# Expert weights in transfers of two chunks instead of one, into the same ring of six slots

## The reference

```python
g, idx = lax.top_k(jnp.swapaxes(aff, 1, 2), cap)
xs = jax.vmap(lambda hb, ib: hb[ib])(h, idx)
a = jnp.einsum("becd,edf->becf", xs, w_gate)
u = jnp.einsum("becd,edf->becf", xs, w_up)
y = jnp.einsum("becf,efd->becd", jax.nn.silu(a) * u, w_down) * g[..., None]
```

## Time and profile before

| | us |
|---|---|
| median of 3 runs | 2307.16 (2306.68 to 2309.15) |
| the profiled execution | 2308.26 |
| its span, first to last instruction | 2306.4 |
| expert stage, first copy to last | about 764 to 2260 |
| TensorE busy | 2116.9 (92%) |
| VectorE busy | 1661.5 (72%) |
| ScalarE busy | 1267.0 (55%) |
| GpSimd busy | 249.9 (11%) |

### The profile page before, as it was taken

How to read it: one execution, slowest core, us unless ns; L and a number is a source line. 1 busy time by engine, 2 the same in 40 slices (tenths; PEclk the granted TensorE clock), 3 DMA queues, 4 the chain that set the end, 5 groups by cost and what they waited for, 6 DMA issues and landing times.

```text
span 2306.4 us, 26811 instructions
## 1 busy us (share of the span) xinstructions
PE 2116.9 (92%) x10228; PEld 1456.2 (63%) x10228; DVE 1661.5 (72%) x1617; ACT 1267.0 (55%) x1271; POOL 249.9 (11%) x100
## 2 busy tenths in 40 slices
PE   7989999897873799999999999999999999999992
PEld 7956576665663466666666666666666666666661
DVE  5013251516333789899899998998989989999885
ACT  0012231404003677777777777777777777777771
POOL 0000000000000202202112021120220211202100
PEclk9989999999885899999999999999999999999996
DMA  6851010101121699999999999999999999999992
GB/s 245 327 191 60 23 59 25 75 9 62 56 97 67 256 384 377 363 398 365 382 387 364 393 371 368 401 362 390 378 365 395 366 378 395 363 390 373 373 353 97
DMA packets 95273, 638.97 MB, mean 277 GB/s; under 512 B 11169, under 2 KB 14400, under 8 KB 21184
## 3 DMA queue, kind: packets, MB, share of 16 engines
q1 hardware_dynamic: 90048, 617.55, 69.0%
q0 software_dynamic: 5120, 19.98, 2.9%
HBM read 619.08 MB, written 18.40 MB: 276 GB/s over the span
## 4 chain that ended last, share of the span: by engine, by line
issue 46%; POOL 9%; DMA 7%; PE 4%; DVE 1%; ACT 0%; POOLq 0%; DVEq 0%; ACTq 0%
DMA place<-x_rows,place 6%; POOL place L889 3%; POOL place L897 2%; POOL acc_rows L901 2%; POOL place L887 2%; PE ps L948 1%; PE ps L943 1%; PE ps L944 1%; PE ps L960 0%; PE ps L965 0%; PE ps L961 0%; DVE place L1034 0%; DVE place L175 0%; DVE place L1059 0%; DVE place L1060 0%
## 5 line engine op out<-in xcount | busy, mean ns | idle before, releaser
L1034 DVE TENSOR_TENSOR place<-ring,place 128x2048 fp32r<-128x2048 f32 x528 | 1283.3, 2436 | 110.2 <-ACT place L995 102.3
L995 ACT ACTIVATE place<-ring 128x2048 fp32r<-128x2048 f32 x528 | 1012.4, 1918 | 373.4 <-PE ps L948 232.8
L943 PE MATMUL ps<-place 128*80 128x512 f32 x1408 | 560.4, 398 | 2.4 <-ACT place L995 2.4
L944 PE MATMUL ps<-place 128*80 128x512 f32 x1408 | 552.8, 393 | 0.0
L948 PE MATMUL ps<-place 128*80 128x512 f32 x1408 | 380.6, 392 | 0.9 <-DVE place L1034 0.9
L948 PEld LDWEIGHTS ps<-place 128*80 128x80 f32 x1408 | 208.2, 148 | 117.0 <-DVE place L1034 2.1
L960 PE MATMUL ps<-place 128*80 128x512 f32 x704 | 280.0, 398 | 0.0
L961 PE MATMUL ps<-place 128*80 128x512 f32 x704 | 276.3, 392 | 0.0
L943 PEld LDWEIGHTS ps<-place 128*80 128x80 f32 x1408 | 208.4, 148 | 107.2 <-issue 3.2
L944 PEld LDWEIGHTS ps<-place 128*80 128x80 f32 x1408 | 209.1, 149 | 104.1 <-issue 0.5
L965 PE MATMUL ps<-place 128*80 128x512 f32 x704 | 191.1, 393 | 0.0
(11 more groups left out here) (138 smaller groups left out, 1702.3 us busy)
## 6 DMA issues: line engine op xcount, KB each, us to landing
ring<-in_w_exp SPq DMA_DIRECT2D x528, 1024.0 KB, 6.9
ring<-in_w_ada SPq DMA_DIRECT2D x24, 1024.0 KB, 6.2
place<-in_w_in SPq DMA_DIRECT2D x12, 1024.0 KB, 6.8
bias_scratch<-place POOLq DMA_DIRECT2D x4, 1024.0 KB, 7.5
ring<-in_w_out SPq DMA_DIRECT2D x4, 1024.0 KB, 4.8
place<-bias_scratch SPq DMA_DIRECT2D x4, 1024.0 KB, 4.8
place<-in_xT SPq DMA_DIRECT2D x1, 2560.0 KB, 22.5
place<-in_x SPq DMA_DIRECT2D x1, 2560.0 KB, 9.4
```

Of the source, the lines that this page charges most:

```text
L943: eng.matmul(out, xH[:, e % 2, kk, :], w, start=(kk == 0), stop=False)
L944: eng.matmul(out, xL[:, e % 2, kk, :], w, start=False, stop=False)
L995: eng.activation(wH[:, n % SPLITS, :], ring[:, (FIRST_EXPERT_CHUNK + n) % RING, :], ACT.Copy).then_inc(wh_done, 1)
L1034: eng.tensor_tensor(wL[:, n % SPLITS, :], ring[:, (FIRST_EXPERT_CHUNK + n) % RING, :], wH[:, n % SPLITS, :].bitcast(F32), ALU.subtract).th ...
```

## The change

Expert chunks are issued in pairs: one DMA of 2 MB fills slots s and s+1, 16 KB in each partition. Since 28 is even and the ring has six slots, a pair's slots are always 4 and 5, 0 and 1, or 2 and 3. The pair waits until both slots are free, that is until chunk n+1-6 has been used, and its landing is told by one semaphore, that of the first slot; whoever waits for either chunk waits for it. Everything else about ring, slots and users stays. The host lays a pair's chunks side by side for each partition. Block 1 now issues the first pair (28, 29), block 3 two pairs, block 4 the rest. As an expert has 33 chunks, pairs begin at even p in even experts and at odd p in odd ones, and piece 32 of an even expert is paired with piece 0 of the next.

```diff
-            src = chunk_source(n) if n < FIRST_EXPERT_CHUNK else a["w_exp"][n - FIRST_EXPERT_CHUNK]
-            eng.dma_start(ring[:, n % RING, :], src).then_inc(landed[n % RING], 16)
+            eng.dma_start(ring[:, n % RING, :], chunk_source(n)).then_inc(landed[n % RING], 16)
+
+        def issue_pair(eng, n):
+
+            eng.wait_ge(chunk_used, n + 1 - RING + 1)
+            s = n % RING
+            eng.dma_start(ring[:, s:s + 2, :].rearrange("p s n -> p (s n)"), a["w_exp"][(n - FIRST_EXPERT_CHUNK) // 2]
+                          ).then_inc(landed[s], 16)
 
         def arrived(eng, n):
+            if n >= FIRST_EXPERT_CHUNK:
+                n -= n % 2
             eng.wait_ge(landed[n % RING], 16 * (n // RING + 1))
...
-                for n in range(RING, ADA_CHUNKS + RING):
+                for n in range(RING, FIRST_EXPERT_CHUNK):
                     issue(eng, n)
+                issue_pair(eng, FIRST_EXPERT_CHUNK)
...
-                for n in range(ADA_CHUNKS + RING, ADA_CHUNKS + RING + OUT_CHUNKS):
-                    issue(eng, n)
+                for n in range(FIRST_EXPERT_CHUNK + 2, FIRST_EXPERT_CHUNK + RING, 2):
+                    issue_pair(eng, n)
...
-                for n in range(ADA_CHUNKS + RING + OUT_CHUNKS, FIRST_EXPERT_CHUNK + EXPERT_CHUNKS):
-                    issue(eng, n)
+                for n in range(FIRST_EXPERT_CHUNK + RING, FIRST_EXPERT_CHUNK + EXPERT_CHUNKS, 2):
+                    issue_pair(eng, n)
...
-    w_exp = np.concatenate([gate_up, down], axis=1).reshape(EXPERT_CHUNKS, P, CW)
+    w_exp = np.concatenate([gate_up, down], axis=1).reshape(EXPERT_CHUNKS // 2, 2, P, CW)
+    w_exp = w_exp.transpose(0, 2, 1, 3).reshape(EXPERT_CHUNKS // 2, P, 2 * CW)
```

## The result

The changed kernel takes 2350.4 us (median of 4 runs, 2345.3 to 2358.1) against 2307.3 before: ratio 1.0188, 95% interval 1.0159 to 1.0217. It is 43 us slower, where I had forecast 7 and a range up to 2334. The profiled execution is the longest of the four, 2358.05 with a span of 2356.2, 49.8 over that of before.

What follows compares the result with a forecast made beforehand. TensorE was taken to bound the expert stage, with no steady-state gain; thin-place stalls summed to 4 to 12 us, taken as +7: 2308.3 + 7 = 2315 profiled, median 2314, range 2304 to 2334.

Steps and rivals of the forecast that it cites:

- What bounds the kernel: Expert stage: TensorE busy all 93.3 us of an expert period, never waiting for weights, so the steady-state gain is nothing.
- Against 5.9 us in the quiet part that is just covered: worth 0 there.: Outside the thin place: some 5 us of lost earliness for a pair's first chunk costs 0, split buffers absorbing 2 us.
- the fourth rival: "The DMA queues become the bound": expert-stage queue holes cost 45 us, 2352; chance 0.08; sign: copies wait in all thirds.
- The thin place: A third into each expert, after scatter and gather, at the hidden product's turn: stalls 0.5 to 1.1 us even, 0 to 0.6 odd.
- The rate of 0.53: In the thin place: VectorE's subtraction runs at 2.28/4.27 = 0.53 of its speed while GpSimd's L889 runs.
- the third rival: "Nothing is given back": GpSimd starts after the stalled subtraction, so thin-place lateness counts in full, 23 us, 2330; chance 0.13.
- The gather: GpSimd's fetch of 80 rows per expert: 16 KB ring rows delay it 0 to 1.5 us, bounds 0 and 5.6.
- the other bound for a pair alone: Landing of a 2 MB pair on a quiet queue: 7.2 us taken, 8.4 with the other bound on the rate.
- The ends that held: Expert 0, the w_in load and the last expert, which has no gather: cost 0; for expert 0 at most 1 us.
- Half as many issues: Sync queue: 528 issues of 0.33 us become 264, worth 0 because that queue waits 1308.4 us anyway.

Runs made afterwards that it cites:

- without arithmetic: Changed kernel with GpSimd's three products and sums cut to 16 of 1024 columns, not computing the reference's values: 2307.3 us, ratio 0.9999.
- its control: Kernel before with GpSimd's three products and sums cut to 16 of 1024 columns, not computing the reference's values: 2300.3 us, ratio 0.9968.
- late issue: Kernel before, single 1 MB transfers, but both of a pair issued only when both slots are free: 2309.8 us, ratio 1.0011.
- late arrival: Kernel before, single 1 MB transfers issued as slots free, but the copy of a pair's first chunk waits for the second's landing: 2309.8 us, ratio 1.0008.
- both late: Kernel before, single 1 MB transfers, issued when both slots are free and first chunk copied only when both have landed: 2344.1 us, ratio 1.0168.
- product first: Hidden product put ahead of VectorE's subtraction, silu ahead of ScalarE's copy: in the changed kernel 2347.7 us (1.0172), in the kernel before with four slots 2395.7 (1.0371).
- without rows: Changed kernel with GpSimd's scatters, and gathers from the third on, replaced by DMAs of 64 bytes a row, not computing the reference's values: 2315.4 us, 1.0037.

## Why the prediction was wrong

*What bounds the kernel* was right: nothing to gain in the steady state, and so was the place in the changed kernel. In the profiled run 26.4 of the 30.3 us of stalls, and all six stretches of half clock, lie directly behind piece 10, at the turn named in the earlier trace rows. With runs of 8 KB, where the gather lands earlier, six of nine stalls lie behind piece 8 instead.

*The step that failed* is "Against 5.9 us in the quiet part that is just covered: worth 0 there." It set a loss of 5.3 us of earliness against a cover that was itself computed with the median landing, left 0.6, and called this enough. It should have asked whether the loop with both effects in it still turns faster than TensorE. My own numbers had it: a pair's landing is the old 6.9 with another 2.5 for its second megabyte, 9.4, and not the 7.2 of a pair alone on the queue; measured 9.7 (and 7.4 at least). With 6.6 to 7 us from the landing to the second subtraction's end that is 16.0 to 16.7 of 17.0. The pair thus came late before the disturbance began: the copies waited in 47 of the 48 thirds of an expert, which I had put down as the sign of the fourth rival.

*The thin place* was priced at 0 to 1.1 us, measured up to 3.6 at one wait. I let GpSimd's slowing of VectorE give most of the lateness back, since a late subtraction would fall behind it. Some came back: the 528 subtractions take 1258.7 us and not 1283.3, 24.6 less, some 1.7 us for each of experts 1 to 14. But in each of these one subtraction was still slowed by 1.5 to 2.0 us, where before two were (1.7 and 2.0), and in expert 5 both were. The rate of 0.53 that I used does not fit the rows, which show the engines taking turns by whole operations. The gather came later too, after 13.3 us in the median instead of 9.6, 3.7 later where I took 0 to 1.5 and allowed 5.6. In expert 5 that is the third rival's mechanism, "nothing is given back"; the loss does not need it, as the next paragraph shows.

*The gather* shows one more term. It lands after 12.8 to 13.9 us in three kernels with runs of 16 KB (changed, eight slots, without arithmetic) and after 9.3 to 10.5 in the eight with 8 KB and the old order of products (before and its control, the 2 MB transfer in two runs, late issue, late arrival, both late, five slots, four slots). With the product first it is 15.6 (16 KB) and 12.1 (8 KB, four slots). The plainest pair is the changed kernel with 13.3 and the same with runs of 8 KB with 10.3: the length of the runs holds the gather back. The queue that carries the weights moves its bytes in 52032 packets in the first and 85824 in the second. That fits the Trainium skill, "DMA: Bandwidth & Descriptors", section "Queues, rings and completion order", by which a DMA engine changes between queues only after a whole packet. But it decided nothing: with 8 KB runs the loss was the same, and with eight slots and a gather nearly as late (12.8) there was none.

*The clock* was not in the sum: some 15 of the 49.8 us of the profiled run are TensorE at half clock behind its stalls.

*A slip in the sum,* without effect: the other bound for a pair alone is 4.7 + 3.1 = 7.8 us and not 8.4, which took the fixed part of one bound and the rate of the other. The shortest landing measured, 7.4, lies near the 7.2 that I used.

*The rivals.* The one whose time came out, 2352 for "the DMA queues become the bound", had the signs right (waits for landings everywhere, a DMA share down from 0.98 to 0.95) and the cause wrong: its holes in the queue are those of a loop with too few slots, and two more slots close them. I had given it 0.08.

*The ends that held:* the w_in load cost nothing (TensorE waited 4.4 us for it, 4.3 before), and none of the 18 stalls lies in the first or the last expert. Half as many issues gained nothing that shows.

## What to carry to other kernels

Before making transfers coarser in a ring of fixed size, add up the loop of one slot group: landing with the queue as loaded as it is, plus everything until the group is free again, against slots times the consumer's time per slot. The coarser unit enters twice, in the landing and in the release, and the loss stays near zero until the sum reaches that limit; here 3 us of spare time cost 1 or 2 us, and 0.3 to 0.6 us cost 37 to 72. A copy that waits for landings all the time without delaying anything is the warning that little of the next disturbance will be absorbed.

## What the runs showed of the hardware that I had not expected

A stall of TensorE in an otherwise full stretch can be followed by 3.4 or 6.8 us at a granted clock of 0.50, and then costs 1.6 to 1.9 times its length: six such stretches in the changed kernel, 34 us in all, behind stalls of 2.8 to 3.6 us. In the kernel before, which has no such stall, the clock is at 1.00 from 771 to 2265 us. In two other kernels a stretch of 3.4 followed a stall of 2.0 us (with runs of 8 KB, at 1655.3; without rows, at 1361.0). The sizes do not order it neatly: a stall of 3.57 us at 1188.2 had 6.8 us of it, one of 2.94 at 1287.9 had 3.4, and in the kernel with both halves late, with 17 stalls of up to 2.9 us, there was one stretch of 3.4. What decides it stays open. Open too is why a pair takes 9.7 us in the median where the quickest takes 7.4; the single transfers before show much the same distance, from 4.7 to 6.9. One part can be seen in the landing semaphores' increments, 16 for each transfer: the first of a pair's comes 7.3 us after the issue (median), the fourteenth 8.9 and the last 9.7 (before 4.8, 6.1 and 6.9). Which engines lag, and behind what, no run here tells.
